# Recurrent gates of a 512-token block: all a gates ahead of the x gates, each output opened by its diagonal tile, the last convolution of a half and the first scan's input in one side bank

## What is computed

```python
def _rglru_mixer(h, w_in, conv_w, conv_b, gate_a_w, gate_a_b, gate_x_w, gate_x_b, lam, w_out):
    gate, xr = jnp.split(h @ w_in, 2, axis=-1)              # D_RNN = 1280 each
    xr = _causal_dwconv(xr, conv_w) + conv_b                # 4 taps
    xh = xr.reshape(b, s, A_HEADS, A_HEAD_DIM)              # 16 heads of 80
    r = jax.nn.sigmoid(einsum("bshi,hij->bshj", xh, gate_a_w) + gate_a_b)
    ig = jax.nn.sigmoid(einsum("bshi,hij->bshj", xh, gate_x_w) + gate_x_b)
    log_a = -LRU_C * r * jax.nn.softplus(-lam)
    a = jnp.exp(log_a)
    u = jnp.sqrt(-jnp.expm1(2.0 * log_a)) * (ig * xr)
    hs = scan of (a, u) along the sequence
    return (hs * gelu(gate)) @ w_out
```

## Time and profile before

| what | value |
|---|---|
| runs | 3106.07, 3106.27, 3099.7 us; median 3106.07 us |
| the profiled execution | 3105.97 us, of which the span of instructions is 3104.0 us |
| mean granted TensorE clock | 0.993 of full speed |
| busy share of the span | PE 98%, PE's weight loads 80%, DVE 45%, ACT 22%, POOL 66% |
| HBM | 303.00 MB read, 98 GB/s over the span |

### The profile page before, as it was taken

The page is one execution under the profiler, slowest core; times in us unless marked ns, Lnnn a source line. Parts: engine busy times, 40 slices in busy tenths (PEclk is TensorE's granted clock), DMA queues, the critical chain, the costliest instruction groups (busy, mean ns, idle before and its releaser), DMA issues.

```text
span 3104.0 us, 38744 instructions
## 1 busy us (share of the span) xinstructions
PE 3040.0 (98%) x13756; PEld 2472.8 (80%) x13756; DVE 1386.5 (45%) x1822; ACT 677.1 (22%) x1191; POOL 2056.8 (66%) x2056
## 2 busy tenths in 40 slices
PE   7999999899999999999999999999999999999998
PEld 4887578688887788888888888888888887888886
DVE  6878732576347654222344222354422256542222
ACT  3255731111003622101122111101200115321110
POOL 4634057566666777777777777787777776777774
PEclk9999999999999999999999999999999999999999
DMA  6711022232222332223322322223222322322221
GB/s 255 273 35 55 8 94 97 76 101 95 95 98 86 102 101 96 95 95 97 107 88 95 100 97 95 95 96 101 95 95 96 100 96 88 102 96 101 95 95 68
DMA packets 85449, 306.86 MB, mean 99 GB/s; under 512 B 9488, under 2 KB 10128, under 8 KB 84944
## 3 DMA queue, kind: packets, MB, share of 16 engines
q1 hardware_dynamic: 82800, 299.30, 28.6%
q10 hardware_dynamic: 2528, 5.83, 0.5%
HBM read 303.00 MB, written 2.10 MB: 98 GB/s over the span
## 4 chain that ended last, share of the span: by engine, by line
PE 92%; DVE 5%; ACT 1%; SPq 1%; DMA 0%; issue 0%; ACTq 0%; DVEq 0%
PE acc L1723 87%; PE acc L823 1%; DVE rec_rec_x L2147 1%; PE side L850 1%; DMA ada_n<-in_ada 0%; PE side L833 0%; SPq L563 0%; PE side L1723 0%; DVE rec_rec_x L2145 0%; PE side L785 0%; PE acc L715 0%; PE stat L1786 0%; DVE att_stat L1494 0%; DVE rec_rec_lo L2154 0%; DVE acc L2133 0%
## 5 line engine op out<-in xcount | busy, mean ns | idle before, releaser
L1685 POOL TENSOR_TENSOR w_lo<-w_raw,w_hi 128x512 fp32r<-128x512 f32 x513 | 668.0, 1302 | 988.0 <-PE acc L1723 962.7
L1723 PE MATMUL acc<-h_hi,w_hi 128*128 128x512 f32 x2224 | 874.9, 393 | 15.0 <-DVE h_lo L1555 8.0
L1723 PE MATMUL acc<-h_lo,w_hi 128*128 128x512 f32 x2224 | 867.7, 390 | 0.0
L1723 PE MATMUL acc<-h_hi,w_lo 128*128 128x512 f32 x2224 | 867.7, 390 | 0.0
L1686 POOL TENSOR_TENSOR w_lo<-w_raw,w_hi 128x512 fp32r<-128x512 f32 x513 | 706.1, 1376 | 0.0
L1723 PEld LDWEIGHTS acc<-h_hi,w_hi 128*128 128x128 f32 x2224 | 418.7, 188 | 112.9 <-issue 15.2
L1723 PEld LDWEIGHTS acc<-h_lo,w_hi 128*128 128x128 f32 x2224 | 419.1, 188 | 85.4 <-issue 1.9
L1723 PEld LDWEIGHTS acc<-h_hi,w_lo 128*128 128x128 f32 x2224 | 418.9, 188 | 85.2
L1674 POOL TENSOR_SCALAR w_hi<-w_raw 128x512 fp32r<-128x512 f32 x513 | 402.1, 784 | 28.4 <-DMA w_raw<-in_weights 28.4
L2116 DVE TENSOR_TENSOR x<-acc,x 128x512 f32 (+1 forms) x160 | 110.7, 692 | 661.8 <-PE acc L1723 661.7
L1723 PE MATMUL acc<-mlp_hid_hi,w_hi 128*128 128x512 f32 x1024 | 398.3, 389 | 0.0
(11 more groups left out here) (358 smaller groups left out, 3495.2 us busy)
## 6 DMA issues: line engine op xcount, KB each, us to landing
w_raw<-in_weights SPq DMA_DIRECT2D x513, 512.0 KB, 3.2
ada<-in_ada SPq DMA_DIRECT2D x36, 512.0 KB, 5.4
ada_more<-in_ada SPq DMA_DIRECT2D x10, 512.0 KB, 15.2
x<-in_x ACTq DMA_DIRECT2D x8, 256.0 KB, 4.7
out<-x SPq DMA_DIRECT2D x8, 256.0 KB, 2.2
x<-in_x ACTq DMA_DIRECT2D x1, 1024.0 KB, 6.3
x<-in_x SPq DMA_DIRECT2D x1, 1024.0 KB, 8.7
ada_n<-in_ada SPq DMA_DIRECT2D x2, 512.0 KB, 15.3
```

Of the source, the lines that this page charges most:

```text
L1685: pool.tensor_tensor(w_lo[:, slot, 0:half], w_raw[:, slot, 0:half], w_hi[:, slot, 0:half].bitcast(F32), ALU.subtract)
L1723: ins = pe.matmul(out, lhs, rhs, start=start, stop=stop, skip_group_check=group)
```

## The change

1. **Order of the gate products on PE.** All five a gates come first, then all five x gates. Each output is opened by its own diagonal tile ("own"); its neighbours' tiles follow in pairs, one "below" the diagonal (input m+1 into output m) and one "above" (input m into output m+1). Two or more outputs are open at once, in different banks. The weights are packed in the same order.
2. **The last convolution of a half** (tile 4 and tile 9) goes into side bank 2 and not into `acc`, with two semaphores of its own (`rec_last_made`, `rec_last_taken`). Each half has one output in `acc` less.
3. **The scan inputs** of tiles 0 and 2 swap places, so that of tile 0 is in side bank 2. In the second half PE waits for the scan of tile 0 before it writes the last convolution there.
4. **VectorE's order**: scan 0 now comes right behind the convolution of tile 7, scans 1 to 4 behind `rec_lo` of tile 9 and ahead of the five `inner` of the second half.
5. **ScalarE's order**: five a sigmoids, then five x sigmoids.

```diff
+GATE_BEGUN = [("a", m) for m in range(HALF)] + [("x", m) for m in range(HALF)]
+GATE_PAIRS = [("a", 0, "own"), ("a", 1, "own"), ("a", 0, "both"), ("a", 2, "own"), ("a", 1, "both"), ("a", 3, "own"),
+              ("a", 2, "both"), ("x", 0, "own"), ("a", 4, "own"), ("a", 3, "both"), ("x", 1, "own"), ("x", 0, "both"),
+              ("x", 2, "own"), ("x", 1, "both"), ("x", 3, "own"), ("x", 2, "both"), ("x", 4, "own"), ("x", 3, "both")]
+GATE_STEPS = [(gate, i, part) for gate, i, kind in GATE_PAIRS for part in (("own",) if kind == "own" else ("below", "above"))]
...
-            return [side[:, 0, :], side[:, 1, :], side[:, 2, :], stat[:, :], M["rec_u"][:, 4, :]]
+            return [side[:, 2, :], side[:, 1, :], side[:, 0, :], stat[:, :], M["rec_u"][:, 4, :]]
...
+        def conv_bank(inst, m):
+
+            return side[:, 2, :] if m % HALF == HALF - 1 else bank(rec_x_out(inst, m))
+
+        def wait_conv_taken(eng, inst, m):
+            if m % HALF == HALF - 1:
+                eng.wait_ge(rec_last_taken, 2 * inst + m // HALF + 1)
+            else:
+                wait_taken(eng, rec_x_out(inst, m))
...
             def recurrent(inst, norm):
+                rec = [(M["rec_hi"][:, k, :], M["rec_lo"][:, k, :]) for k in range(RT)]
+
+                def last_conv(half):
+
+                    if half:
+                        pe.wait_ge(rec_scan, RT * inst + 1)
+                    out = side[:, 2, :]
+                    for k, (hi, lo) in enumerate(h_parts):
+                        slot, cols = next_tile()
+                        mm(out, w_hi[:, slot, cols], hi, k == 0, False)
+                        mm(out, w_hi[:, slot, cols], lo, False, False)
+                        ins = mm(out, w_lo[:, slot, cols], hi, False, k == KT - 1)
+                    ins.then_inc(rec_last_made, 1)
+
+                def gate_products(half):
+
+                    outs = {}
+                    begun = iter(GATE_BEGUN)
+                    for gate, i, kind in GATE_STEPS:
+                        slot, cols = next_tile()
+                        m = HALF * half + i
+                        if kind == "own":
+                            while (gate, i) not in outs:
+                                outs[next(begun)] = begin_out()
+                            wait_conv_taken(pe, inst, m)
+                        if kind == "below":
+                            wait_conv_taken(pe, inst, m + 1)
+                        out = outs[gate, i + 1] if kind == "above" else outs[gate, i]
+                        hi, lo = rec[m + 1] if kind == "below" else rec[m]
+                        ends = kind == "below" or kind == "above" and i == HALF - 2
+                        mm(out, w_hi[:, slot, cols], hi, kind == "own", False)
+                        mm(out, w_hi[:, slot, cols], lo, False, False)
+                        ins = mm(out, w_lo[:, slot, cols], hi, False, ends)
+                        if ends:
+                            ins.then_inc(out_made, 1)
+
                 for half in range(2):
                     for m in range(HALF):
+                        if m == HALF - 1:
+                            last_conv(half)
+                            continue
                         project(h_parts, ready_h(norm) if half == 0 and m == 0 else None)
                         if half == 0 and m == 0:
                             norm_sum(norm)
                             if inst == 0:
                                 pe.wait_ge(own_summed, KT)
                                 pe.matmul(side[:, 0, :], ones[:, :], square[:, 0, :], start=True, stop=True).then_inc(own_stat, 1)
-                    for m in range(HALF * half, HALF * half + HALF):
-                        for gate in range(2):
-                            project([(M["rec_hi"][:, k, :], M["rec_lo"][:, k, :]) for k in BD[m]],
-                                    lambda i, m=m: wait_taken(pe, rec_x_out(inst, BD[m][i])))
+                    gate_products(half)
                     skip_to_panel()
                 for m in range(RT):
...
-                def gates(o, m):
-                    wait_made(act, o)
-                    act.activation(M["rec_a"][:, m, :], bank(o), ACT.Sigmoid,
-                                   bias=col("a_gate_a_b", RT * inst + m)).then_inc(out_taken[o % BANKS], 1)
-                    wait_made(act, o + 1)
-                    act.activation(bank(o + 1), bank(o + 1), ACT.Sigmoid,
-                                   bias=col("a_gate_x_b", RT * inst + m)).then_inc(rec_ig, 1)
+                def gates(o, half):
+
+                    for i in range(HALF):
+                        m = HALF * half + i
+                        wait_made(act, o + i)
+                        act.activation(M["rec_a"][:, m, :], bank(o + i), ACT.Sigmoid,
+                                       bias=col("a_gate_a_b", RT * inst + m)).then_inc(out_taken[(o + i) % BANKS], 1)
+                    for i in range(HALF):
+                        m, x_o = HALF * half + i, o + HALF + i
+                        wait_made(act, x_o)
+                        act.activation(bank(x_o), bank(x_o), ACT.Sigmoid,
+                                       bias=col("a_gate_x_b", RT * inst + m)).then_inc(rec_ig, 1)
...
                 for m in range(HALF):
                     if m == HALF - 1:
-                        conv_low(o + m - 1, m - 1)
-                    convolved(o + m, m)
+                        conv_low(m - 1)
+                    convolved(m)
                     if 0 < m < HALF - 1:
-                        conv_low(o + m - 1, m - 1)
-                conv_low(o + HALF - 1, HALF - 1)
-                o += HALF
-                gates = [o, o + 3 * HALF]
+                        conv_low(m - 1)
+                conv_low(HALF - 1)
+                o += HALF - 1
+                gates = [o, o + 3 * HALF - 1]
                 for i in range(HALF):
-                    inner(o + 2 * i + 1, i)
+                    inner(o + HALF + i, i)
                 o += 2 * HALF
-                convolved(o, HALF)
+                convolved(HALF)
                 for i in range(3):
                     ratio(first, i)
-                conv_low(o, HALF)
-                convolved(o + 1, HALF + 1)
+                conv_low(HALF)
+                convolved(HALF + 1)
                 for i in range(3, HALF):
                     ratio(first, i)
-                conv_low(o + 1, HALF + 1)
-                for i in range(2, HALF):
-                    if i == HALF - 1:
-                        conv_low(o + i - 1, HALF + i - 1)
-                    convolved(o + i, HALF + i)
-                    if 2 < i < HALF - 1:
-                        conv_low(o + i - 1, HALF + i - 1)
-                conv_low(o + HALF - 1, 2 * HALF - 1)
-                o += HALF
+                conv_low(HALF + 1)
+                convolved(HALF + 2)
+                scanned(first, 0, gates[0])
+                conv_low(HALF + 2)
+                convolved(HALF + 3)
+                conv_low(HALF + 3)
+                convolved(HALF + 4)
+                conv_low(HALF + 4)
+                o += HALF - 1
+                for i in range(1, HALF):
+                    scanned(first, i, gates[0])
                 for i in range(HALF):
-                    inner(o + 2 * i + 1, HALF + i)
-                    scanned(first, i, gates[0])
+                    inner(o + HALF + i, HALF + i)
                 o += 2 * HALF
```

More of the change, by code:

```diff
@@ L265, in build @@
         rec_conv = sem("rec_conv")
+        rec_last_made = sem("rec_last_made")
+        rec_last_taken = sem("rec_last_taken")
         rec_hi_made = sem("rec_hi_made")
@@ L1974, in recurrent @@
                 for m in range(HALF):
[L1975 to L1976 removed]
+                    conv_high(m)
+                o += HALF - 1
                 act.wait_ge(rec_cl_made, 3)
[L1978 to L1979 removed]
+                gates(o, 0)
                 decays(first, o)
                 o += 2 * HALF
[L1982 removed]
+                conv_high(HALF)
                 roots(first, range(0, 3))
[L1984 removed]
+                conv_high(HALF + 1)
                 roots(first, range(3, HALF))
                 for i in range(2, HALF):
[L1987 to L1990 removed]
+                    conv_high(HALF + i)
+                o += HALF - 1
+                gates(o, 1)
                 decays(first + HALF, o)
@@ L2149, in convolved, with conv_low @@
                                .then_inc(rec_conv if back == A_TAPS - 1 else rec_tap, 1)
-                def low(o, m, hi_count):
-                    dve.wait_ge(rec_hi_made, hi_count)
-                    dve.tensor_tensor(M["rec_lo"][:, m, :], bank(o), M["rec_hi"][:, m, :].bitcast(F32), ALU.subtract)\
-                       .then_inc(out_taken[o % BANKS], 1)
-                def conv_low(o, m):
-                    low(o, m, 2 * first + m + 1)
+                def conv_low(m):
+                    dve.wait_ge(rec_hi_made, 2 * first + m + 1)
```

(23 more changed lines are left out.)

43 lines of the change are left out of this document (17 added, 26 removed).

## The result

The changed kernel takes **3107.2 us** (median of 17 runs, 3104.2 to 3112.6) against 3103.8 us for the kernel before in the same set of runs: ratio 1.0014, 95% interval 1.0008 to 1.0021, that is 2.5 to 6.5 us more. Two of the 17 executions of the kernel before took 4545.6 and 5318.8 us and are left out of the ratio. The forecast was 3109 and a shift of +3.2 us. The profiled execution took 3107.2 us (span 3105.1).

What follows compares the result with a forecast made beforehand. TensorE was taken as the bound, busy 3040.0 of 3104.0 us, so only its instructions, waits and clock matter. Two layers at -0.2 + 1.8 = +1.6 us each add 3.2 to 3105.97: 3109 us, range 3103 to 3113.

Steps and rivals of the forecast that it cites:

- the sum: Whole kernel: two recurrent layers, each -0.2 + 1.8 = +1.6 us, so +3.2 us on 3105.97, giving 3109 us.
- First half: Gate stage of each recurrent layer's first half: a wait for ScalarE's second a sigmoid replaces that for `rec_lo`, gaining 0.2 us.
- I let each behave as its predecessor: First halves: new waits keep the old ones' clock behaviour, a fall after 1.76 us and none after 1.42 us.
- Table load: ScalarE's switch to sigmoid: 1.31 us taken from the rows; the skill's 2.66 us would have given 3114.6 us.
- Second half: Each recurrent layer's second half: PE waits 3.3 us for scan 0 with a clock fall; the stage loses 1.8 us.
- Wait for a1: Second half's gates: after ten tiles PE waits about 1 us for ScalarE to take the second a gate.
- some 5 us into tile 9's old slot: Sign of being right: scan 0's `rec_scan` ends some 5 us into the last convolution's old slot on PE.
- the clock fall behind the scan's wait: PE's last convolution in the second half: low clock after the 3.3 us wait, costing 1.5 us.
- Rival (a): Waits before the first x gate: the clock falls at three more of them, 3113.7 us; chance 0.10.
- Rival (b): Second halves: no clock fall after the waits for scan 0, 3105.7 us; chance 0.12.
- Rival (c): Neither scan 0 nor the second a gate is ever awaited; the whole 12.7 us goes, 3093.3 us; chance 0.06.
- The scans ahead of the x gates' products: VectorE, second half: four remaining scans moved ahead of 7.5 us of x gate products, claimed to cost nothing.

Runs made afterwards that it cites:

- t7: The change with only the sigmoid table loaded ahead of each half's last copies, filler set for the new tile: 3105.1 us, ratio to before 1.0005.
- u4: The change run again, unchanged: 3108.3 us, ratio to the kernel before 1.0017.
- u3: The change with only s3's order of convolutions and `rec_lo` on VectorE, scan 0 staying behind tile 7's convolution: 3108.3 us, ratio to before 1.0016.
- t6: As t5, with the products of x gates 0 to 2 of the second half placed behind scans 2 to 4: 3093.9 us, ratio to before 0.9974.
- s3: As s2, with VectorE's convolutions of tiles 7, 8 and 9 ahead of `rec_lo` of 7 and 8: 3100.1 us, ratio to before 0.9990.
- t5: As s3, with a one-column sigmoid loading the table ahead of each half's last copies, its tile counted in the filler: 3097.7 us, ratio to before 0.9983.
- s1: The change with scan 0's input in SBUF, so PE waits for `rec_ratio` in place of the scan: 3112.9 us, ratio to before 1.0035.
- u1: The kernel before with an unused one-column tile ahead of the filler, shifting everything behind it by 32 bytes: 3135.7 us, ratio 1.0110.
- u2: The kernel before with an unused 16-column tile ahead of the filler, shifting everything behind it by 64 bytes: 3116.4 us, ratio 1.0047.
- t8: The kernel before, its gate order and banks kept, with s3's VectorE order and t5's table load: 3098.2 us, ratio 0.9988.
- s2: As s1, with scan 0 moved behind `rec_lo` of tile 9, among scans 1 to 4: 3109.1 us, ratio to before 1.0019.

## Why the prediction was right, and where it was off

The forecast's mechanism and sign held: the waits came where they were put, at nearly the forecast lengths. The time is 2 us from the forecast, and that close for reasons that are partly luck (see the sum).

- **First half.** The forecast was a gain of 0.2 us from a wait for a1 in place of that for `rec_lo`. Layer 0: 19.24 us for the stage against 19.41, with a wait of 1.28. Layer 3: 19.58 against 21.39. Here the step "I let each behave as its predecessor" failed: the clock did not fall behind 1.62 us, in neither profile of the change, which is 1.6 us of gain that the sum did not have.
- **Table load.** 1.31 us by rows 5, and 1.41 us when it was taken off the path (t7). The 2.66 us that the Trainium skill ("ScalarE: Activation LUTs", "What ACT_TABLE_LOAD costs") gives with its drain, and the 3114.6 us worked out from it, did not come.
- **Second half.** Wait for scan 0: forecast 3.3, measured 3.12 and 3.12. Start of tile 8 on VectorE: forecast 1036.91, which is 1034.65 on the new trace's clock (its second half starts 2.26 us earlier, 1009.12 against 1011.38); measured 1034.61. Wait for a1: forecast about 1, measured 1.00 twice. The sign "some 5 us into tile 9's old slot" for the end of scan 0 does not fit the prediction's own sum, 1036.38 - 1033.14 = 3.2 us; measured it is 3.1.
- **The term that was mis-sized most is the clock fall behind the scan's wait.** I took 1.5 us from falls behind 2.5 us of idleness. It cost 2.8 and 1.7 us here, 3.0 and 1.8 in u4, 1.8 and 2.9 in t7, 0.15 and 1.7 in u3: a mean of 2.0 over eight equal waits. The loss per second half was therefore 3.2 and 2.0 us in place of 1.8.
- **The sum.** These two errors nearly cancel: +3.0 us in layer 0 and +0.2 in layer 3 in the profiled pair, +3.2 as forecast, though spread otherwise. The profiled execution of before had also caught a fall at 966 us (1.7 us) that has nothing to do with the change and that the one after did not have. By the larger set of runs before is 3103.8 us, not 3106.1, so the same shift from there gives 3107. The forecast stood on an execution of before that had all of its falls; other executions have fewer (they reach down to 3099.5 us), so the loss between typical ones is larger than forecast, 4.3 and 5.3 us by the ratios of the two sets of the change. Too high a start and too small a shift partly cancel in 3109.
- **Rival (a)** did not come: no clock fall behind any of x0's waits. **Rival (b)** fell to the windows above; of eight waits for scan 0 in four profiles one, in u3, was without a fall. **Rival (c)**, 3093.3 us, needed the table loaded ahead of the copies or scan 0 ahead of tile 7. t6, which loads the table ahead, puts scan 0 behind tile 9 and has no long wait left, takes 3093.9 us, but the likeness is luck: it is 8.7 us below the kernel before beside it, about the 8.2 us of waits, and not the 12.7 us that count every fall as well. The scans ahead of the x gates' products cost nothing in the change, as forecast, but 0.9 to 1.5 us per layer as soon as PE came earlier (s3, t5; 0.34 in t7).

## What to carry to other kernels

Moving a wait off one buffer only pays if what is late next is moved as well: price the engine that makes the next operand, in its order, before reordering TensorE. Here the change alone cost 3 to 6 us, repairs tried one by one brought 2 to 3 us (t7), nothing (u3) or a further loss of some 5 (s1), and all of them together won 9 against the kernel before. A function switch of ScalarE belongs ahead of the last work that doesn't need it. After any new tile in SBUF, compare the mean ns of matmuls that the edit did not touch.

## What was not expected of the hardware

- **Addresses.** With all tiles behind the new one shifted by 32 bytes, a 128x512 fp32 matmul that streams one of them took 395 ns in place of 389, 33 us over the program (u1); by 64 bytes, 389 to 395 by operand, 14 us (u2). This kernel's filler is written to keep them at multiples of 256 bytes (`LINE`). What in the address matters was not tested further.
- **VectorE beside GpSimd.** The product and scan of s1, with both inputs in SBUF, took 1.11 and 2.20 us while GpSimd was busy throughout with weight panels, and GpSimd's second row below took 1.75 us in place of the 1.29 of the first:

```profile
1033.18 1.29 POOL L1693 TENSOR_TENSOR w_lo<-w_raw,w_hi 128x512 fp32r<-128x512 f32 x1 [1.26 <-PE side L1731]
1034.42 1.75 POOL L1694 TENSOR_TENSOR w_lo<-w_raw,w_hi 128x512 fp32r<-128x512 f32 x1
```

  The change's scan 0 (1.22 us at 1032.89, above) is no fair comparison, since GpSimd did nothing during it. Scan 1 of the change, with its input in a side bank, ran beside GpSimd, and scan 4 of s1, with its input in SBUF, while GpSimd did nothing (VectorE and GpSimd of the change, then VectorE of s1):

```profile
1049.09 1.22 DVE L2230 TENSOR_TENSOR_SCAN rec_rec_x<-rec_rec_a,side 128x512 f32<-128x512 f32 x1
```

```profile
1048.49 1.29 POOL L1693 TENSOR_TENSOR w_lo<-w_raw,w_hi 128x512 fp32r<-128x512 f32 x1 [1.79 <-PE acc L1731]
1049.74 1.28 POOL L1694 TENSOR_TENSOR w_lo<-w_raw,w_hi 128x512 fp32r<-128x512 f32 x1
```

```profile
1055.44 1.22 DVE L2230 TENSOR_TENSOR_SCAN rec_rec_x<-rec_rec_a,rec_rec_u 128x512 f32<-128x512 f32 x1
```

  So neither the input in SBUF nor GpSimd alone makes the scan long; both together do. The Trainium skill, "SBUF — State Buffer", section "🔬 SBUF: two separate sides", says that a VectorE operation with two SBUF inputs and a GpSimd operation that reads SBUF exclude each other; the trace agrees in that both slow down (1.22 to 2.20 us and 1.29 to 1.75 us) and that neither does when one input of the scan is in PSUM. So scan 0's side bank, which made the wait, also keeps the scan at 1.22 us when GpSimd is at work.
- **The clock.** Equal waits at the same place are followed by a fall in one execution and not in another: behind 1.88 us of idleness near 966 us in 6 of 14 profiles (1.7 us in each of the five that can be compared), behind 3.12 us in 7 of 8, behind the old order's waits of 2.50 and 2.49 us in both, and behind its 2.41 and 2.42 us in u2 in neither. The Trainium skill, "TensorE: Matmul & The Clock Gate", section "Part 1: The HAM clock gate", says that the number of slow matmuls changes from run to run with the phase in which a kernel meets the gate; these profiles agree for falls behind short waits: the two equal waits for scan 0 in u4 cost 3.0 and 1.8 us, those in u3 0.15 and 1.7. A single profile can't price a fall; the number and length of the waits can be compared, and they repeat.

The lowest times are a way around the falls. The table sets the lowest time of each kernel against the lowest of before in the same set of runs, and PE's waits in the two recurrent layers (from the profile) against the 8.2 us of before, in us:

| kernel | lowest time | waits |
|---|---|---|
| s3 | -2.0 | -1.9 |
| t8 | -1.8 | -1.2 |
| t5 | -5.1 | -5.0 |
| t6 | -8.3 | -8.0 |
| the change | +4.5 | +3.0 |
| the change again (u4) | +3.8 | +3.0 |
| u3 | +3.6 | +2.6 |
| t7 | +1.2 | -1.0 |
| s2 | +5.2 | +3.3 |
| s1 | +10.9 | +6.7 |

Where no wait is longer than 2 us (the first four rows) the lowest time follows the waits within 0.7 us. Where there are two waits of 3.12 to 5.24 us (the others) it lies 0.8 to 4.2 us above them, which fits that nearly all such waits had a fall of 1.7 to 3.0 us in the profiles. This is an estimate from the lowest of 5 to 32 executions each, not a measurement of one execution.
